# A decoder block with a PEER expert layer: four late groups instead of two, whole value rows, seven units marked ahead

## The reference, cut to what matters

```python
s = jnp.einsum('bshpd,hpnd->bshpn', q, sub_keys)          # 8 heads, 2 halves, 128 keys each
top_v, top_i = lax.top_k(s, PEER_TOPK)                    # 16 of each half
cand = top_v[..., 0, :, None] + top_v[..., 1, None, :]
cand_v, cand_i = lax.top_k(cand, PEER_TOPK)               # 16 of the 256 pairs
experts = i1 * PEER_NKEYS + i2
gates = jax.nn.softmax(cand_v, axis=-1)
act = jax.nn.gelu(jnp.einsum('td,tkd->tk', xb, u_tab[eb]))
out = jnp.einsum('tk,tkd->td', gb * act, v_tab[eb])       # v_tab: 16384 rows of 8 kB
```

## Time and profile before

| what | number |
|---|---|
| median of three runs | 2982.83 us |
| profiled execution, its span | 2985.51 us, 2983.8 us |
| busy in the span | PE 78%, DVE 69%, ACT 44%, POOL 20% |
| read from HBM | 692.11 MB, 233 GB/s over the span |
| dot stage, groups 0 to 13 | from 1577.8 to 2207.8 us |
| units of the second token tile | from 2214.3 to 2265 us |
| value stage, 256 steps | from 2270.3 to about 2970 us |

### The profile page before, as it was taken

The page is one execution under the profiler, slowest core; times in us unless marked ns, Lnnn a source line. Parts: engine busy times, 40 slices in busy tenths (PEclk is TensorE's granted clock), DMA queues, the critical chain, the costliest instruction groups (busy, mean ns, idle before and its releaser), DMA issues.

```text
span 2983.8 us, 43098 instructions
## 1 busy us (share of the span) xinstructions
PE 2342.1 (78%) x15833; PEld 2179.0 (73%) x15833; DVE 2065.4 (69%) x2730; ACT 1313.0 (44%) x1888; POOL 605.3 (20%) x383
## 2 busy tenths in 40 slices
PE   6999999999999999998893000022338999999998
PEld 6999999999999999998893000012236888888886
DVE  6775456666547445543669999999985677777774
ACT  4564544444444434443441000067885444444443
POOL 0000000000001000100005766766743112111110
PEclk8999999999999999999897555555569999999999
DMA  6444565545665655544466999999943888888885
GB/s 198 141 142 135 176 183 156 158 152 150 195 177 156 190 183 180 182 140 141 127 226 281 386 366 373 385 394 375 384 179 106 288 304 320 304 314 309 311 290 168
DMA packets 338997, 695.78 MB, mean 233 GB/s; under 512 B 24792, under 2 KB 266672, under 8 KB 301376
## 3 DMA queue, kind: packets, MB, share of 16 engines
q1 hardware_dynamic: 296080, 386.19, 40.8%
q0 software_dynamic: 42304, 307.25, 25.6%
q10 hardware_dynamic: 496, 0.84, 0.1%
HBM read 692.11 MB, written 2.10 MB: 233 GB/s over the span
## 4 chain that ended last, share of the span: by engine, by line
PE 72%; DVE 22%; ACT 3%; issue 2%; POOL 1%; DMA 1%; ACTq 0%; DVEq 0%; POOLq 0%
PE bank L375 42%; PE bank L1431 23%; DVE b_u_ring L1841 14%; PE bank L1240 1%; PE bank L1125 1%; PE bank L1407 1%; DVE b_w_lo L357 1%; DVE b_rstd L419 1%; ACT b_spread L991 1%; PE bank L1326 1%; PE bank L1308 0%; POOL b_u_ring L648 0%; DVE b_scr L436 0%; ACT b_w_hi L352 0%; ACT b_col_ring L1000 0%
## 5 line engine op out<-in xcount | busy, mean ns | idle before, releaser
L357 DVE TENSOR_TENSOR b_w_lo<-b_raw,b_w_hi 128x1024 fp32r<-128x1024 f32 x464 | 569.9, 1245 | 533.3 <-ACT b_w_hi L352 532.7
L352 ACT ACTIVATE b_w_hi<-b_raw 128x1024 fp32r<-128x1024 f32 x464 | 485.1, 1057 | 616.6 <-PE bank L375 607.4
L375 PE MATMUL bank<-b_act_hi,b_w_hi 128*128 128x256 f32 x1920 | 548.7, 286 | 12.1 <-DVE b_w_lo L357 9.2
L375 PE MATMUL bank<-b_act_lo,b_w_hi 128*128 128x256 f32 x1920 | 545.3, 284 | 0.0
L375 PE MATMUL bank<-b_act_hi,b_w_lo 128*128 128x256 f32 x1920 | 545.1, 284 | 0.0
L1841 DVE CUSTOM_DVE_ANT_0 b_u_ring<-b_u_ring,b_xnN 128x2048 f32<-128x2048 f32 x220 | 488.4, 2288 | 1.7 <-DMA b_u_ring<-in_peer_u,b_idx_all 1.7
L648 POOL DMA_INDIRECT b_u_ring<-in_peer_u,b_idx_all x220 | 414.6, 1884 | 251.4 <-DVE b_dots L1841 133.2
L1864 DVE TENSOR_TENSOR b_v_lo<-b_v_raw,b_v_hi 128x1024 fp32r<-128x1024 f32 x256 | 312.5, 1224 | 219.2 <-ACT b_v_hi L1040 216.6
L1040 ACT ACTIVATE b_v_hi<-b_v_raw 128x1024 fp32r<-128x1024 f32 x256 | 271.7, 1062 | 399.1 <-PE bank L1431 320.4
L375 PEld LDWEIGHTS bank<-b_act_hi,b_w_hi 128*128 128x128 f32 x1920 | 370.5, 193 | 15.6 <-DVE b_w_lo L357 7.8
L375 PEld LDWEIGHTS bank<-b_act_lo,b_w_hi 128*128 128x128 f32 x1920 | 370.7, 193 | 0.1
(11 more groups left out here) (301 smaller groups left out, 3696.1 us busy)
## 6 DMA issues: line engine op xcount, KB each, us to landing
b_v_raw<-in_peer_v SPq DMA_DIRECT2D x256, 512.0 KB, 6.1
b_raw<-in_w_in SPq DMA_DIRECT2D x208, 512.0 KB, 3.9
b_raw<-in_w_proj_dsa SPq DMA_DIRECT2D x32, 512.0 KB, 3.6
b_raw<-in_w_proj_gla SPq DMA_DIRECT2D x32, 512.0 KB, 3.5
b_raw<-in_w_xk SPq DMA_DIRECT2D x32, 512.0 KB, 3.7
b_raw<-in_w_out SPq DMA_DIRECT2D x32, 512.0 KB, 3.4
b_raw<-in_w_xv SPq DMA_DIRECT2D x32, 512.0 KB, 4.3
b_raw<-in_w_xq SPq DMA_DIRECT2D x32, 512.0 KB, 4.5
```

Of the source, the lines that this page charges most:

```text
L352: act.activation(w_hi[:, q], raw[:, UQ * c + q], ACT.Copy).then_inc(w_high, 1)
L357: dve.tensor_tensor(w_lo[:, q], raw[:, UQ * c + q], w_hi[:, q].bitcast(F32), ALU.subtract).then_inc(w_split, 1)
L375: mm = pe.matmul(proj[c][:, n], lhs, rhs, start=(q == 0 and n == 0 and k == 0 and t == 0), stop=(q == UQ - 1 and k == UK - 1 and t == 2), ...
```

## The change

**Late groups.** Four groups (12 to 15) are late instead of two. The dot stage ends with group 11. The value stage takes 128 late rows instead of 64: the first at step 26 instead of 24, the last at step 234 instead of 232. The two places of `late_row` and the wait of the gathers stay as they were.

**Routes.** The routes of groups 14 and 15 had stood behind the dots of groups 11 and 12. They now stand, with their gate exponentials, behind the weigh of group 10.

**Marks ahead.** Units 0 to 6 get places of their own (`row_ahead`, `col_ahead`). ACT marks them (`mark_unit`) in groups 4 to 6, for which the indices are turned earlier (a `turn_tables` of its own, once `routed` is 8). After the weights of group 7 only the scaling and the copying of these units are left. ACT then makes 11 units in the turn of group 7 and 7 in each of groups 8, 9 and 10, where it had made 4, 6, 6, 6, 6 and 4 in groups 7 to 12.

**Values.** A load brings a whole tile of 128 rows of 8 kB (1 MB, two steps). There are two places, and a third from tile 32 (step 64) on, in the part of `spread` that is used up by then.

```diff
-LATE = tuple(range(GROUPS - 2, GROUPS))
+LATE = tuple(range(GROUPS - 4, GROUPS))
-LATE_STEP = 24
+LATE_STEP = 26
+THIRD_TILE = 32
+MADE_AHEAD = 7
...
+    row_ahead = [sb(f"row_ahead{n}", [UNIT, NKEYS], SCR + n * 2 * K if n < 4 else WRK + (4 + 2 * (n - 4)) * K)
+                 for n in range(MADE_AHEAD)]
+    col_ahead = [sb(f"col_ahead{n}", [UNIT, NKEYS], WRK + (10 + 2 * n) * K) for n in range(3)]
-    v_raw = [sb(f"v_raw{n}", [VCOLS], (HT if n < 2 else WRK + 4 * K) + n % 2 * 4 * K + n // 2 * 4 * K) for n in range(4)]
+    v_raw = [sb(f"v_raw{n}", [D], at) for n, at in enumerate((HT, WRK + 8 * K, RAW + 72 * K))]
...
+        if 4 <= u < MADE_AHEAD:
+            return col_ahead[u - 4]
+    def row_at(u):
+        return row_ahead[u] if u < MADE_AHEAD else row_hot[:, u % ROWS_HELD]
...
+    def value_place(j):
+        return j % 2 if j < THIRD_TILE else (j - THIRD_TILE + 2) % 3
+    def value_landed(j):
+        return v_landed[value_place(j)], 16 * [value_place(i) for i in range(j + 1)].count(value_place(j))
+    def raw_half(n):
+        return v_raw[value_place(n // 2)][:, n % 2 * VCOLS:(n % 2 + 1) * VCOLS]
...
-        def load_values(b, first=False):
-            for n in range(4 * BATCH):
-                if not (first and n < 4):
-                    apart(sem("v_split"), b * 4 * BATCH + (n - 3))
-                rows = v_rows[bass.ds(b * 2 * BATCH * P + n // 2 * P, P)]
-                sp.dma_start(v_raw[n % 4], rows[:, n % 2 * VCOLS:(n % 2 + 1) * VCOLS]).then_inc(v_landed[n % 4], 16)
-        load_values(0, first=True)
-        with sp.Fori(1, NKEYS // (2 * BATCH)) as b:
-            load_values(b)
-        sp.wait_ge(sem("v_split"), 2 * NKEYS - 2)
+        for j in range(NKEYS):
+            if j == 1:
+                sp.wait_ge(sem("unit_spread"), MADE_AHEAD)
+            if j == THIRD_TILE:
+                sp.wait_ge(sem("e_split"), 2 * THIRD_TILE // PER_BATCH)
+            elif j >= 2:
+                sp.wait_ge(sem("v_split"), 2 * (j - (2 if j < THIRD_TILE else 3)) + 2)
+            sp.dma_start(v_raw[value_place(j)], v_rows[j * P:(j + 1) * P]).then_inc(value_landed(j)[0], 16)
+        sp.wait_ge(sem("v_split"), 2 * NKEYS)
...
-        def make_unit(u):
-            row = row_hot[:, u % ROWS_HELD]
-            wait(act, sem("unit_spread"), u - ROWS_HELD + 1)
+        def mark_unit(u):
+            row = row_at(u)
+            if u >= MADE_AHEAD:
+                wait(act, sem("unit_spread"), u - ROWS_HELD + 1)
+        def make_unit(u):
+            row = row_at(u)
+            if u >= MADE_AHEAD:
+                mark_unit(u)
...
-            act.wait_ge(v_landed[n % 4], n // 4 * 16 + 16)
+            act.wait_ge(*value_landed(n // 2))
-            act.activation(v_hi[:, n % 2], v_raw[n % 4], ACT.Copy).then_inc(sem("v_high"), 1)
+            act.activation(v_hi[:, n % 2], raw_half(n), ACT.Copy).then_inc(sem("v_high"), 1)
...
-        with act.Fori(1, 8) as g:
+        for g in range(1, 8):
-        turn_over(0, (0, 3))
+            if g == 4:
+                act.wait_ge(sem("routed"), PEER_H)
+                turn_over(0, (0, 2))
+            if g == 4:
+                act.wait_ge(sem("seeded"), 1)
+            if g in (4, 5, 6):
+                for u in range(2 * (g - 4), 2 * (g - 4) + 2 + g // 6):
+                    mark_unit(u)
+        turn_over(1, (2, 3))
-            for u in range(made, min(made + (4 if g == 7 else 6), UNITS // 2)):
+            if g == EARLY - 2:
+                for late in range(g + 4, GROUPS):
+                    gate_exp(late)
+            for u in range(made, min(made + (MADE_AHEAD + 4 if g == 7 else 7), UNITS // 2)):
-        turn_over(1, (0, 2))
+        turn_over(2, (0, 2))
-        turn_over(2, (2, 3))
+        turn_over(3, (2, 3))
...
+        pe.wait_ge(sem("routed"), PEER_H)
+        turn_tables(0, (isel_all[:, 0], isel_all[:, 1]), 0, 0)
-        turn_tables(0, (isel_all[:, 0], isel_all[:, 1], w_all), 0, 0)
+        turn_tables(1, (w_all,), 0, 0)
-        turn_tables(1, (isel_all[:, 0], isel_all[:, 1]), 1, UNITS // 2)
+        turn_tables(2, (isel_all[:, 0], isel_all[:, 1]), 1, UNITS // 2)
-        turn_tables(2, (w_all,), 1, UNITS // 2)
+        turn_tables(3, (w_all,), 1, UNITS // 2)
...
+            if g == EARLY - 2:
+                for late in range(g + 4, GROUPS):
+                    route(late)
-        dve.wait_ge(sem("tables_turned"), 3)
+        dve.wait_ge(sem("tables_turned"), 4)

```

More of the change, by code:

```diff
@@ L535, in hybrid_block @@
     u_landed = [sem(f"u_landed{s}") for s in range(RING)]
-    v_landed = [sem(f"v_landed{s}") for s in range(4)]
+    v_landed = [sem(f"v_landed{s}") for s in range(3)]
     w_in = a["w_in"][0]
@@ L652, in pool_cols @@
         def pool_cols():
-            pool.wait_ge(sem("tables_turned"), 2)
+            pool.wait_ge(sem("tables_turned"), 3)
             for u in cols_of("pool"):
@@ L1023, in turn_over @@
             lo, hi = tables
-            at = slice(0, P) if n == 0 else slice(P, T)
+            at = slice(0, P) if n < 2 else slice(P, T)
             act.activation(turned[:, lo:hi, at], bank[0][:, 0:(hi - lo) * P].rearrange("p (n t) -> p n t", n=hi - lo), ACT.Copy
@@ L1406, in spread_unit @@
             for k in range(UNIT):
-                mm = pe.matmul(bank[u % 2][:, k * P:(k + 1) * P], col_at(u)[:, k], row_hot[:, u % ROWS_HELD, k], start=True,
-                               stop=True)
+                mm = pe.matmul(bank[u % 2][:, k * P:(k + 1) * P], col_at(u)[:, k], row_at(u)[:, k], start=True, stop=True)
             mm.then_inc(sem("unit_spread"), 1)
@@ L1863, in value_low @@
                 dve.wait_ge(sem("v_used"), n - 3)
-            dve.tensor_tensor(v_lo[n % 4], v_raw[n % 4], v_hi[:, n % 2].bitcast(F32), ALU.subtract).then_inc(sem("v_split"), 1)
+            dve.tensor_tensor(v_lo[n % 4], raw_half(n), v_hi[:, n % 2].bitcast(F32), ALU.subtract).then_inc(sem("v_split"), 1)
         def weights_low(b):
```

## The result

| | before | after |
|---|---|---|
| median of the runs (us) | 2983.95 (2982.5 to 2985.32, 4 runs) | 3036.82 (3027.5 to 3049.33, 4 runs) |
| profiled execution, its span (us) | 2985.51, 2983.8 | 3038.21, 3036.5 |

The ratio is 1.0185 with a 95% interval of 1.0168 to 1.0201: the change makes the kernel slower by 53 us. The prediction had slower, 3065 us and a range of 2950 to 3115.

The account below looks back on a forecast made before the run. DVE was taken to bound the dot stage and PE the value stage, where late-row gathers would then set the pace. 2985.5 - 53.8 + 136 = 3067.7, less 2.7 for the median: 3065 us, range 2950 to 3115.

Parts of the forecast that it names:

- What leaves the dot stage: Dot stage: two groups of dots leave, ACT makes three more units behind route 15; second token tile 53.8 us earlier.
- Marks ahead at nothing: Groups 4 to 7: marking seven units early fits ACT's turns of 44.8 us, so it costs nothing.
- The way of a late row: Value stage: two places turn over in 11.2 us at best, 8.9 wanted; gathers set the pace, +136 us.
- the 8.4: Value stage: microseconds from a late row's gather issue to its last packet, the mean of three gathers before the change.
- whole value rows, costed at nothing: Value stage: refilling whole-tile places takes 7.7 us against 8 to 10 available, fits barely, so no cost.
- Late rows land in time: Rival, value stage: gathers come quickly enough, steps keep 2.73 us, only the front counts; 2929 to 2955 us, chance 0.15.
- The bytes: Rival, value stage: 243 MB in 208 steps bound it, +6 to +64 us, 2935 to 2993 us; chance 0.07.
- More goes wrong: Rival, value stage: two value places starve (19 to 38 us) or the clock falls (+107 us); above 3115 us, chance 0.08.

Follow-up runs that it names:

- tiny tiles: The changed kernel with all but three of the 128 value tiles loading only 256 bytes of each row; 2956.7 us, ratio 0.9923 to the kernel before.
- half loads: The changed kernel with each value tile loaded as two transfers of half rows (4 kB) into the same places; 3114.72 us, ratio 1.0449 to the kernel before.
- run 3115: Not a run number but the time of half loads, the changed kernel with each value tile loaded as two transfers of half rows; measured 3114.72 us.
- half use: The changed kernel with DVE's late dots and sums on the first half of each late row, gathers and loads full size; 3059.63 us, ratio 1.0256.
- half use with tiny tiles: The changed kernel with DVE's late operations on half a row and value tiles loading 256 bytes a row; 2930.34 us, ratio 0.9832.
- half tiles: The changed kernel with only the first half of each value row loaded (512 KB a tile) and used for both halves; 3046.12 us, ratio 1.0216.
- four places: The changed kernel with four places for late rows instead of two, from the 37th late row on; 2973.14 us, ratio 0.997 to the kernel before.
- two value places: The changed kernel without the third place for value tiles, two places to the end; 3027.97 us, ratio 1.0157 to the kernel before.
- three groups: The changed kernel with three late groups instead of four, two places for late rows; 2957.61 us, ratio 0.9905 to the kernel before.

## Why the prediction was right in direction and 28 us too high

**What leaves the dot stage: right.** -53.8 us forecast, -58.0 measured. 4 us of it were there before the change acts: the first dot of the stage began at 1573.9 us instead of 1577.8, and the route behind group 7's dots at 1935.14 instead of 1939.14. That is scatter: in the traces of all kernels shown here this first dot comes between 1571.9 and 1578.8 us. The rest, -54.0, is the forecast. ACT and not DVE keeps the difference: 21.1 us of idle ahead of the weigh, 20 forecast.

**Marks ahead at nothing: right.** In the timeline of ACT a unit that was marked ahead costs 2.1 us, a scaling and a copy (seven of them from 1945.5 to 1960.2), and the 11 units of group 7's turn end at 1983.0, just as the table of the next gelu is loaded:

```profile
1956.23 1.24 ACT L1040 ACTIVATE b_row_ahead<-b_row_ahead,b_turned 128x128 f32<-128x128 f32 x4
1957.37 1.08 ACT L1008 ACTIVATE b_spread<-bank 128x512 f32<-128x512 f32 x1
1958.21 1.25 ACT L1040 ACTIVATE b_row_ahead<-b_row_ahead,b_turned 128x128 f32<-128x128 f32 x4
...
1981.98 1.03 ACT L1008 ACTIVATE b_spread<-bank 128x512 f32<-128x512 f32 x1
1983.03 1.28 ACT L1056 ACT_TABLE_LOAD   x1
1984.32 0.22 ACT L1056 ACTIVATE b_gelu<-b_dots 128x16 f32<-128x16 f32 x1
```

The gelu waits for nothing there. Without the marks that stage loses 22 us.

**The way of a late row: the right bound, a term too large.** The mechanism is shown from four sides: more places (-64 us), fewer late rows (-79), a shorter way (tiny tiles, -80, where half the bytes alone gave nothing) and a longer one (half loads, +78). In the changed kernel 105 of 126 rows are used within 1.0 us of their last packet; before, DVE began 6.9 us after it on average. The sizes: hold 2.65 (2.57 forecast), way 7.34 (8.4), until used 0.67 (0.2); a turn of 10.66 us, not 11.2. Over 63.5 turns the shorter way is 67 us less than forecast, and 30 us come back because DVE begins later than the 0.2 us allowed. With the hold's 0.1 us and small roundings (63 turns instead of 63.5, 568 us before instead of 565.0) the stretch grew by 111.7 instead of 136 us; the front's 4 us are the rest of the 28. So two misses of opposite sign brought the total near, and that is luck. The step that failed is that of the 8.4, taken from rows that ran beside half-row loads, together with "whole value rows, costed at nothing". They were no cost but a gain: beside half loads the way is 8.7 us under this load and the run 3115 us, 50 above the forecast; beside whole loads it is 7.3. The prediction looked at whole rows only for what they do to ACT, and not for what they do to the other queue.

Of the mean of 7.34 there are two kinds. In 44 of 128 gathers the first packet comes within 2.6 us and the last after 6.1 on average; in 61 it comes after more than 4.5 us and the last after 8.3. The difference is a tile in front: the gather issued at 2641.74 could have begun at 2644.1 by the 2.4 us of tiny tiles, and this is what the queues did in 2644.2 to 2646.7 us of the changed kernel:

```profile
q1 hardware_dynamic: 116, 0.95, 94.0%
q0 software_dynamic: 3, 0.00, 0.1%
```

It starts at 2646.75, when the tile's packets are through. The Trainium skill (DMA: Bandwidth & Descriptors, Queues, rings and completion order) has an engine drain a whole packet of some 9 to 17 descriptors of one ring before it turns to the next. A tile's 128 rows over 16 engines are 8 each, and the packets of the tile run through before the row's begin, so this trace agrees. In half use it does not everywhere: from 2644.64 us on packets of a row and of a tile start by turns, 0.31 us apart, which is what each lasts.

**Rivals.** *Late rows land in time* didn't happen; its price was good: half use with tiny tiles, where they do, runs at 2930 us, 2929 was forecast. The Trainium skill's sum (the same page, Anatomy of one DMA: 2.0 us and the bytes over 436 GB/s, an estimate of 4.4 us) is short even in tiny tiles, where the way is 6.0 us: 2.4 to the first packet and 3.6 for 1.05 MB. *The bytes* are not the bound of the changed kernel (half tiles); with four places 422 GB/s are moved and they may be the next one. *More goes wrong* didn't happen in its size: ACT waited 58.6 us for tiles where it had waited 55.8, and even the 299 us with two value places didn't lengthen the run. The clock did fall a little: PE is busy 605.7 us where 565.0 did before, at a mean clock of 0.96 instead of 1.00, so 90% of the stretch and not the 81% of the forecast. Since most late rows are used as soon as they are there, that should lie inside the time that DVE waits for rows, but no run separates the two.

**What stays open.** Why half use lets the packets of rows and tiles run into each other, while in the changed kernel they mostly follow one another, wasn't settled. It is probably a matter of when each is issued; half use with tiny tiles shows only that the tiles' packets are what does it. Nor is it settled why the way was 8.3 us with three groups and two places, and 8.9 with four places.

## What to carry to other kernels

A ring of few places has a turn: hold, way, and the time until the consumer begins. Work it out before more work is sent through it. The way must be taken from rows beside the traffic that there will be, not that there was: size and timing of the other queue's transfers moved it here from 5.6 to 8.8 us with two places. A stream that is short of places is mended by more places (-64 us) or by less work: with two places three groups gain 25 us where four lose 53, and four places add at most 6 us to that. So how much work is moved is to be chosen by the turn.

## What the runs showed that was not expected

- Half the bytes in the other queue changed next to nothing (7.34 and 7.54 us for the way), and almost none brought only 1.3 us. With half of them the first packet came 0.8 us earlier and the last 0.9 us later after it.
- With four groups and two places, loads of 1 MB in 8 kB packets let a row through better than the same bytes in 4 kB packets: 3.6 instead of 5.0 us from a late row's first packet to its last, and a 1 MB load landed in 5.0 us where one of 512 KB took 7.5. The size of a load alone isn't it (in half tiles, with half as many 512 KB loads, one took 5.7), nor do 8 kB packets ensure it (5.0 us from first to last in half use).
- A shorter hold made the kernel 23 us slower (half use), and only as long as the tiles' packets were there.
